# Four blocks on one core: the first two weight chunks of a layer split ahead, row blocks transposed at the old layer's end

## What is computed

```python
for l in range(2):                       # the hybrid layers
    h = rms_norm(x, pre_g[l])
    p = h @ w_in[l] + b_in[l]            # 16 column groups
    mix = concat(stick_breaking(p), sparse(p), forgetting(p), latent(p)) * silu(gates)
    x = x + rms_norm(mix @ w_out[l], post_g[l])
x = x + attention_ab(rms_norm(x, ln_ab) @ w_in_ab) @ w_out_ab
x = x + attention_c(rms_norm(x, ln_c) @ w_in_c) @ w_out_c
return rms_norm(x, ln_f)
```

## Time and profile before

| what | value |
|---|---|
| time, three runs | median 1887.13 us (1882.69 to 1889.14) |
| time of the profiled execution | 1885.34 us |
| its span, first to last instruction | 1883.3 us |
| its mean granted TensorE clock | 0.996 |
| TensorE matmul busy | 1857.6 us, 99% |
| VectorE busy | 1011.1 us, 54% |
| ScalarE busy | 859.5 us, 46% |
| DMA | 338.99 MB, mean 180 GB/s |

### The profile page before, as it was taken

How to read it: one execution, slowest core, us unless ns; L and a number is a source line. 1 busy time by engine, 2 the same in 40 slices (tenths; PEclk the granted TensorE clock), 3 DMA queues, 4 the chain that set the end, 5 groups by cost and what they waited for, 6 DMA issues and landing times.

```text
span 1883.3 us, 22540 instructions
## 1 busy us (share of the span) xinstructions
PE 1857.6 (99%) x9566; PEld 1590.7 (84%) x9566; DVE 1011.1 (54%) x987; ACT 859.5 (46%) x1066; POOL 163.2 (9%) x168
## 2 busy tenths in 40 slices
PE   8999999999999999999999999999999999999998
PEld 6889988898788998889878888888888888888886
DVE  5545454474663455457465555455455555555544
ACT  5344443464543445346445443354354434435443
POOL 2300011000340001000020000010000101100011
PEclk9999999999999999999999999999999999999999
DMA  9665555455566455446556555455556555456553
GB/s 313 201 193 153 157 189 169 145 182 190 191 203 205 144 172 191 149 140 205 170 176 197 183 192 189 161 184 175 182 179 200 179 167 184 146 172 201 174 184 112
DMA packets 187156, 338.99 MB, mean 180 GB/s; under 512 B 6848, under 2 KB 48688, under 8 KB 186160
## 3 DMA queue, kind: packets, MB, share of 16 engines
q1 hardware_dynamic: 181536, 316.89, 51.8%
q0 software_dynamic: 5232, 20.59, 3.9%
q10 hardware_dynamic: 288, 0.07, 0.0%
HBM read 335.43 MB, written 2.10 MB: 179 GB/s over the span
## 4 chain that ended last, share of the span: by engine, by line
PE 92%; DVE 3%; ACT 2%; DMA 1%; issue 1%; ACTq 0%; DVEq 0%
PE acc L1503 27%; PE acc L1505 27%; PE acc L1504 27%; PE bank L1656 3%; DVE w_lo L975 2%; PE bank L1596 1%; DMA raw<-in_w_in 1%; PE bank L1625 1%; PE bank L1645 1%; PE bank L1860 1%; PE bank L1586 1%; PE bank L1759 1%; ACT w_hi L641 1%; PE bank L1614 0%; DVE x L1299 0%
## 5 line engine op out<-in xcount | busy, mean ns | idle before, releaser
L975 DVE TENSOR_TENSOR w_lo<-raw,w_hi 128x2048 fp32r<-128x2048 f32 (+4 forms) x304 | 668.1, 2200 | 581.6 <-ACT w_hi L641 581.6
L1503 PE MATMUL acc<-w_hi,xt_hi 128*128 128x512 f32 (+4 forms) x2432 | 923.6, 380 | 8.5 <-DVE w_lo L975 8.3
L1505 PE MATMUL acc<-w_hi,xt_lo 128*128 128x512 f32 (+4 forms) x2432 | 915.7, 377 | 0.0
L1504 PE MATMUL acc<-w_lo,xt_hi 128*128 128x512 f32 (+4 forms) x2432 | 915.2, 376 | 0.0
L641 ACT ACTIVATE w_hi<-raw 128x2048 fp32r<-128x2048 f32 (+4 forms) x304 | 549.6, 1810 | 614.7 <-PE acc L1505 591.9
L1503 PEld LDWEIGHTS acc<-w_hi,xt_hi 128*128 128x128 f32 x2432 | 457.4, 188 | 89.4 <-DVE w_lo L975 7.0
L1505 PEld LDWEIGHTS acc<-w_hi,xt_lo 128*128 128x128 f32 x2432 | 457.3, 188 | 80.7
L1504 PEld LDWEIGHTS acc<-w_lo,xt_hi 128*128 128x128 f32 x2432 | 457.6, 188 | 78.7 <-issue 0.5
L716 ACT ACTIVATE S<-S,nmax 128x256 f32<-128x256 f32 (+1 forms) x128 | 59.9, 469 | 74.9 <-DVE nmax L1067 49.9
L515 POOL DMA_DIRECT2D bias<-in_b_in x32 | 18.0, 562 | 613.8 <-DVE M L1055 209.9
L703 ACT ACTIVATE PT<-bank 128x512 f32<-128x512 f32 (+2 forms) x76 | 36.3, 554 | 69.7 <-PE bank L1645 51.8
(11 more groups left out here) (279 smaller groups left out, 1192.6 us busy)
## 6 DMA issues: line engine op xcount, KB each, us to landing
raw<-in_w_in SPq DMA_DIRECT2D x76, 1024.0 KB, 5.1
raw<-in_w_in_c SPq DMA_DIRECT2D x64, 1024.0 KB, 5.5
raw<-in_w_in_ab SPq DMA_DIRECT2D x52, 1024.0 KB, 5.1
raw<-in_w_out SPq DMA_DIRECT2D x32, 1024.0 KB, 5.1
raw<-in_w_out_ab SPq DMA_DIRECT2D x16, 1024.0 KB, 5.0
raw<-in_w_out_c SPq DMA_DIRECT2D x16, 1024.0 KB, 5.0
raw<-in_w_in SPq DMA_DIRECT2D x16, 688.0 KB, 4.0
raw<-in_w_in SPq DMA_DIRECT2D x16, 576.0 KB, 3.8
```

The costliest lines, as they stand in the source:

```text
L975: nc.vector.tensor_tensor(w_lo[r][:, :, 0:n], raw[r][:, :, 0:n], w_hi[r][:, :, 0:n].bitcast(F32), ALU.subtract).then_inc(lo_done.s, 1)
L1503: nc.tensor.matmul(s, xt_hi[:, kt, rows], w_hi[r][:, k, 0:n], start=(q == 0 and k == 0), stop=False)
L1504: nc.tensor.matmul(s, xt_hi[:, kt, rows], w_lo[r][:, k, 0:n], start=False, stop=False)
L1505: ins = nc.tensor.matmul(s, xt_lo[:, kt, rows], w_hi[r][:, k, 0:n], start=False, stop=(q == NQ - 1 and k == KQ - 1))
```

## The change

- The first two chunks of layers 1 and 2 (AB) get places of their own, `ahead`. Pair 0 lies in the memory of `TQ, TK, TV, CT`, pair 1 in that of `QT, KT, ukv, QR, mla_g`. They may be written when the old layer's last slot has done its first step. Their splits move from the last slot's stages to those of the slot before it. The other chunks go on through the ring of three.
- The loads of `mla_g` and `ukv`, whose memory pair 1 uses, move behind the first slot on GpSimd's queue, in both hybrid layers.
- Row blocks (0, 2) and (0, 3) are transposed at the end of the old layer's last slot.
- The first slot does all four chunks for t = 0, then all four for t = 1. The blocks of t = 1 are transposed after its steps 2, 3 and 4 (counted from 0).
- On ScalarE and VectorE the row blocks stand elsewhere between norm, x updates and splits.

```diff
+AHEAD = 2
...
+        def ahead_pair(i):
+            with ExitStack() as scope:
+                return [scope.enter_context(nc.sbuf_tensor(f"ahead_{part}{i}", [P, KQ, CW], F32R)) for part in ("hi", "lo")]
...
         w_lo = [sb(f"w_lo{r}", [P, KQ, CW], F32R) for r in range(RING)]
+        ahead = [ahead_pair(0)]
         TQ, TK, TV = sb("TQ", [P, T, GW]), sb("TK", [P, T, GW]), sb("TV", [P, T, GW])
         CT = sb("CT", [P, T, GW])
...
+        ahead.append(ahead_pair(1))
         with ExitStack() as hybrid:
...
-        def must_be_used(i):
-            j = i - RING
-            return j + 1 - min(max(j + 1 - NQ * CMP_SLOT, 0), NQ)
+        def weights(turn, i):
+            if turn and i < AHEAD:
+                return ahead[i]
+            r = (i - AHEAD * turn) % RING
+            return w_hi[r], w_lo[r]
+        def place_free(turn, i):
+            if turn and i < AHEAD:
+                return split_used(turn, -RING)
+            used = i + 1 - RING - (AHEAD if turn and i < AHEAD + RING else 0)
+            if turn < DEPTH:
+                used -= min(max(used - NQ * CMP_SLOT, 0), NQ)
+            return split_used(turn, used)
...
-        SPLITS_AFTER = {-1: NQ - 1, CMP_SLOT - 1: NQ - 2, CMP_SLOT: NQ + 2, H_SLOTS - 2: NQ - 2, H_SLOTS - 1: RING}
+        SPLITS_AFTER = {-1: NQ - 2, CMP_SLOT - 1: NQ - 2, CMP_SLOT: NQ + 2, H_SLOTS - 2: NQ - 2 + AHEAD, H_SLOTS - 1: NQ - AHEAD}
...
-        FIRST_SLOT = [(q, (t,)) for t in range(T) for q in range(RING)] + EVENLY[RING:]
+        FIRST_SLOT = [(q, (t,)) for t in range(T) for q in range(NQ)]
...
@@ gpsimd
+                nc.gpsimd.dma_start(fbias[:, :], ...)
+                nc.gpsimd.dma_start(uq, ...)
+                pool.wait_ge(*tr_lo(l, 8))
+                nc.gpsimd.dma_start(gT[:, :], ...)
+                next_bias(0)
                 nc.gpsimd.dma_start(mla_g[:, 0:MLA_QR], all_rows(q_g[bass.ds(l, 1), :])).then_inc(small_in.s, 16)
                 nc.gpsimd.dma_start(mla_g[:, MLA_QR:GW], all_rows(kv_g[bass.ds(l, 1), :])).then_inc(small_in.s, 16)
-                nc.gpsimd.dma_start(fbias[:, :], ...)
-                nc.gpsimd.dma_start(uq, ...)
                 nc.gpsimd.dma_start(ukv[:, :], flat(w_ukv)).then_inc(mlaw_in.s, 16)
-                pool.wait_ge(*tr_lo(l, 8))
-                nc.gpsimd.dma_start(gT[:, :], ...)
-                next_bias(0)
...
@@ scalar, split_hi
-                r = i % RING
+                hi, _ = weights(turn, i)
                 act.wait_ge(*arrived(turn, i))
-                act.wait_ge(*split_used(turn, must_be_used(i) if turn is not DEPTH else i + 1 - RING))
-                nc.scalar.activation(w_hi[r][:, :, 0:n], raw[r][:, :, 0:n], ACT.Copy).then_inc(hi_done.s, 1)
+                act.wait_ge(*place_free(turn, i))
+                nc.scalar.activation(hi[:, :, 0:n], raw[i % RING][:, :, 0:n], ACT.Copy).then_inc(hi_done.s, 1)
...
@@ scalar and vector, first_rows
-                rows_t(turn, 0, 3)
-                for v in range(3):
-                    rows_t(turn, 1, v)
+                rows_t(turn, 1, 0)
+                rows_t(turn, 1, 1)
                 yield
+                rows_t(turn, 1, 2)
                 rows_t(turn, 1, 3)
-                yield
...
@@ scalar, hybrid_after, last slot of a layer
+                            if t == 0:
+                                row_root(l, t, "eps6")
+                            rows_t(l + 1, 0, 2 * t)
+                            rows_t(l + 1, 0, 2 * t + 1)
                             if t:
-                                yield
-                            row_root(l, t, "eps6")
-                            for v in range(2 if t == 0 else 0):
-                                yield
-                                rows_t(l + 1, 0, v)
-                            if t:
-                                rows_t(l + 1, 0, 2)
+                                row_root(l, t, "eps6")
+                            yield
...
@@ vector, hybrid_after, last slot of a layer
                         output_mean(l, t, 1e-6)
+                        if t:
+                            rows_t(l + 1, 0, 2)
+                            rows_t(l + 1, 0, 3)
                         output_norm(l, t)
                         for v in range(2):
+                            if t and v:
+                                yield
                             d = slice(CW * v, CW * v + CW)
                             nc.vector.scalar_tensor_tensor(x[:, t, d], M[:, t, d], stat[:, 14 + t:15 + t], x[:, t, d],
                                                            ALU.mult, ALU.add).then_inc(x_done.s, 1)
-                            if t and v == 0:
-                                rows_t(l + 1, 0, 2)
-                                yield
...
-                        for v in range(2 if t == 0 else 0):
+                        if t == 0:
+                            rows_t(l + 1, 0, 0)
+                            rows_t(l + 1, 0, 1)
                             yield
-                            rows_t(l + 1, 0, v)
...
@@ tensor, layer_starts
-                for v in range(2):
+                for v in range(N_OUT):
                     drained[v] = tr_lo(turn, v + 1)
...
-                after = {0: some((0, 2), (0, 3)), 1: some((1, 0)), 2: some((1, 1), (1, 2)), 3: some((1, 3))}
+                after = {2: some((1, 0)), 3: some((1, 1), (1, 2)), 4: some((1, 3))}
...
@@ tensor, last slot of a layer
-                        halfway, after = {step: lambda: rows_t(l + 1, 0, 0)}, {step: lambda: rows_t(l + 1, 0, 1)}
+                        def last_rows():
+                            rows_t(l + 1, 0, 2)
+                            rows_t(l + 1, 0, 3)
+                        halfway = {step: lambda: rows_t(l + 1, 0, 0)}
+                        after = {step: lambda: rows_t(l + 1, 0, 1), step + 1: last_rows}
```

More of the change, by code:

```diff
@@ L537, in _ @@
                 next_bias(0)
+                nc.gpsimd.dma_start(mla_g[:, 0:MLA_QR], all_rows(q_g[bass.ds(l, 1), :])).then_inc(small_in.s, 16)
+                nc.gpsimd.dma_start(mla_g[:, MLA_QR:GW], all_rows(kv_g[bass.ds(l, 1), :])).then_inc(small_in.s, 16)
+                nc.gpsimd.dma_start(ukv[:, :], flat(w_ukv)).then_inc(mlaw_in.s, 16)
                 rope(TQ[:, :, :].rearrange("p t (h n) -> p t h n", n=HD), "rope", P,
@@ L875, in _ @@
             for l in range(DEPTH):
-                i = RING if l else PIECED
+                i = NQ
                 for k in range(-1, H_SLOTS):
-                    todo = SPLITS_AFTER.get(k, NQ) + (RING - PIECED if l == 0 and k == -1 else 0)
+                    todo = SPLITS_AFTER.get(k, NQ)
                     for _ in hybrid_after(l, k):
@@ L946, in _ @@
             for turn, (_, _, slot0, slots, stages, _, _) in zip((DEPTH, DEPTH + 1), SECTIONS):
[L947 removed]
+                i = NQ * slot0 + (RING if turn > DEPTH else NQ)
                 last = N_CHUNKS2 if turn == DEPTH + 1 else 10 ** 9
                 for k in range(-1, len(slots) + N_OUT):
[L950 removed]
+                    todo = {-1: NQ - (1 if turn > DEPTH else 2), len(slots) + N_OUT - 1: 1}.get(k, NQ)
                     for _ in att_after(turn, k, slots, stages):
@@ L1502, in slot @@
                             s = acc[a % 2][t][:, 0:n]
-                            nc.tensor.matmul(s, xt_hi[:, kt, rows], w_hi[r][:, k, 0:n], start=(q == 0 and k == 0), stop=False)
-                            nc.tensor.matmul(s, xt_hi[:, kt, rows], w_lo[r][:, k, 0:n], start=False, stop=False)
-                            ins = nc.tensor.matmul(s, xt_lo[:, kt, rows], w_hi[r][:, k, 0:n], start=False,
+                            nc.tensor.matmul(s, xt_hi[:, kt, rows], hi[:, k, 0:n], start=(q == 0 and k == 0), stop=False)
+                            nc.tensor.matmul(s, xt_hi[:, kt, rows], lo[:, k, 0:n], start=False, stop=False)
+                            ins = nc.tensor.matmul(s, xt_lo[:, kt, rows], hi[:, k, 0:n], start=False,
                                                    stop=(q == NQ - 1 and k == KQ - 1))
@@ L1510, in slot @@
                         ins.then_inc(split_used.s, 1)
-                    elif q == NQ - 1:
+                    elif q == NQ - 1 and order is LAST_SLOT:
                         ins.then_inc(rows_done.s, 1)
```

22 lines of the change are left out of this document (9 added, 13 removed).

## The result

The changed kernel takes **1878.17 us** (median of 4 runs, 1877.12 to 1879.30), beside 1887.31 for the kernel before (4 runs, 1882.69 to 1889.14): ratio **0.9958**, 95% interval 0.9946 to 0.9970. Run again on another occasion it took 1879.24 (5 runs) beside 1885.01 (21 runs of the kernel before): ratio 0.9968, 0.9956 to 0.9981. So it is faster by 0.3 to 0.4%. The profiled execution took 1878.3 us, its span is 1876.5; before they were 1885.34 and 1883.3. The trace thus holds 7.0 us in time and 6.8 in span, and those have to be placed.

The account below looks back on a forecast made before the run. TensorE, busy 99% of the span, was taken as the bound, leaving only its waits and slow clock to win. Boundaries 6.35 us plus start 1.2 made 7.6, so 1879.5 us against the median, range 1873 to 1887.

Parts of the forecast that it names:

- Case A: Whole kernel: boundaries gain 6.35 us and the start 1.2, giving 1879.5 us, own range 1873 to 1882; chance 0.57.
- rival B: First slot: VectorE stands behind GpSimd's multiply and add, TensorE waits 1.7 us; 1881.7, or 1885.1 with clock lost; chance 0.20.
- start, the wait at 49: First layer's second slot: with ukv's load moved, the 1.22 us low-part wait goes, gaining 1.2 us, bounds 0 and 1.22.
- first boundary, gain: End of first layer: waits and slow clock fall from 4.2 us to 1.05.
- second boundary, gain: End of second layer: waits and slow clock fall from 4.1 us to 0.9.
- wait at the first block (square late): Old layer's end: square some 0.3 us late, so TensorE waits 0.15 us at the first boundary, none to 0.15 at the second.
- wait before the fourth step: First slot: TensorE waits 0.6 us for chunk 3's low part, bounds nothing and 1.7 us.
- gap before the seventh step: First slot: block (1,2) ready late behind chunk 4's low part, 0.3 us, bounds 0 and 1.1.
- The price of the boundary before: Old kernel's layer boundaries: low-part waits plus 1.72 us of slow clock cost 4.2 and 4.1 us, together 8.3.
- rival C: Old layer's end: ScalarE is held by the second early load landing late, from about 7 us; 1895 us; chance 0.10.
- the low part of chunk 3: First slot, VectorE: 2.34 us behind a 1.63 us x update, done at 501.5 where TensorE asks at 500.9.
- D: After the first slot or at the start: gain given back, only one part stays, 1.2 us, 1885.9; chance 0.13.

Follow-up runs that it names:

- e1: Kernel before with only the loads of mla_g and ukv moved behind the first slot on GpSimd: 1883.93 us, ratio 0.9992.
- e5: Changed kernel, but GpSimd begins its x update of row tile 1 only after chunk 3's low part: 1876.41 us, repeated at 1877.01.
- e7: Changed kernel with one more GpSimd multiply, result unused, ahead of its update of row tile 1: 1877.92 us in one run.
- e3: Changed kernel with the splits of chunks 0 and 1 back among the last slot's stages: 1894.40 us, ratio 1.0048.
- e2: Changed kernel with the first slot's old order, chunks 0 to 2 per row tile, then chunk 3: 1892.78 us, ratio 1.0040.
- e6: Changed kernel with GpSimd's later update, plus all four row-tile-1 blocks before chunk 4's split on ScalarE and VectorE: 1876.43 us, ratio 0.9955.
- e4: Changed kernel with row blocks (0,2) and (0,3) transposed after the new slot's first step again: 1885.02 us, ratio 0.9997.

## Why the prediction was right, point by point

**The forecast case.** 1879.5 us was said against the median of the kernel before, 7.6 us less; the median is 1878.17, and the profiled span gives 6.8. That the time came within 1.3 us owes something to the base: by medians the gain is 9.1 us on the first occasion and 5.8 on the second, where the kernel before had 1885.01. The forecast of 7.6 lies between them. Case A happened in its boundaries and its clock, but one of its steps went as rival B had it, as is said below. The table of the steps is:

| step of the sum | forecast | measured |
|---|---|---|
| start, the wait at 49 | 1.2 | 1.39 (alone, in `e1`: 1.38) |
| first boundary, gain | 3.15 | 2.93 |
| second boundary, gain | 3.2 | 2.53 |
| wait at the first block (square late) | 0.15 | none seen (square 0.03 late) |
| wait before the fourth step | 0.6 | 1.00 and 0.99 |
| gap before the seventh step | 0.3 | 0.23 |

**The price of the boundary before was right.** The 2.3 us waits and the slow clock are what went. The second boundary's 1.72, which I had only carried over from the first, can be counted: eight starts from 982.37 to 985.89 in 3.52 us where 1.82 would do, 1.70. By the waits the second boundary should have given 4.04 less 1.22, 2.8 us; it gave 2.53, and the last 0.3 I can't place.

**The early splits were priced right, their lateness too high.** The second load landed about 4.9 us after its issue, against the 5.1 I took, so its high part began at 477.78, that is 479.17 on the time scale of before (1.39 added) and not 479.4. That is most of why the square was 0.03 instead of 0.3 us late. That rival C's condition (a landing over 7 us) was far off is seen in the 1.07 us wait before the second high part.

**The term that was mis-sized: the low part of chunk 3.** I gave it 2.34 us, so 0.6 of wait, on the ground that "the same two instructions meet the same two of GpSimd as before". They did not: before, the four row-block instructions stood between the update and the low part, and GpSimd's add (to 498.92) was over when the low part began, 498.74, but for 0.2 us. Now the low part comes directly behind the update, at 497.35, with GpSimd's add just begun (496.95 to 498.57), and has 3.38 us. The wait was 1.00. The range of that term, 0 to 1.7, held it.

It was luck that the miss stayed so small. A low part 1.04 us longer than forecast should have made the wait 1.6, above the 1.39 up to which I had seen the clock kept. On the time scale of before the x update began at 497.18 and not at 497.5, and TensorE asked at 501.17 and not at 500.9; these two took 0.6 us off again.

**The reading that was wrong: how the two engines meet.** I argued from the overlap of the records that VectorE and GpSimd "slowed each other rather than queue". `e5` and `e7` show that they queue. The record of an instruction that stands behind the other engine's has its wait inside: the x update is 0.74 us of work (0.75 in `e5`) in a record of 1.63, and the low part is 2.28 in one of 3.38. Two records that overlap say nothing about sharing. The ends in the changed kernel go the same way as in `e7`: multiply 496.87, update 497.42 (0.55 later, as there), add 498.57 (1.15, as there), low part 500.73 (2.16, there 2.14). In the kernel before, too, the multiply ends at 497.23 and the update at 497.78, 0.55 later: the rows that I read as sharing held the turns.

The Trainium skill (SBUF — State Buffer, on port contention) states that a VectorE instruction with two SBUF inputs and a GpSimd instruction that reads SBUF exclude each other for a whole instruction. It was right where my row reading spoke against it: the low part of 3.38 in the changed kernel, 2.28 in `e5` and 3.12 in `e7` agree with it.

So rival B named the mechanism and case A did not. B let the low part begin at the end of GpSimd's add, about 500.3, and end at 502.6. On the same time scale the add ended at 499.96 and the low part at 502.12. B's price was 0.7 us too dear, a wait of 1.7 for 1.00: the low part ended 0.48 earlier than B had it, and TensorE asked 0.27 later. With 1.00 the clock stayed, and the time came out on A's side.

**The clock.** The forecast took it that waits of 1.22 and 1.39 us keep the clock and 2.32 lose it. In the changed kernel this held: 1.00 us of wait, clock 1.00 behind both. As a rule it is too strong: 1.84 us lost it in `e3`, 2.02 kept it in `e2`, 2.32 kept it once in `e1`, and the 1.39 us at 590 to 600 lost it in `e5`, in its repeat and in `e6`, and kept it in the other eight profiles (before, changed, again, `e1`, `e2`, `e3`, `e4`, `e7`). The step of the prediction that was exposed to this is the 2 x 1.72 us of its gain. The prediction's sign of a clock of 1.00 throughout held at the boundaries only: the fall at 222, which the kernel before has too, is still there.

**The rivals.** C did not happen: the square was not late. D did not: between the boundary and 591 TensorE has no idle record, and what was gained at the first boundary is still there at the second. The whole of the 6.8 us stays to the end.

**What may lie beyond.** `e5` (1876.41 and 1877.01 us) and `e6` (1876.43) have no boundary wait. In spans they are 1874.1 to 1875.6 against 1876.5 and 1877.2 of the changed kernel; in medians 1 to 3 us under it, with overlapping intervals (ratios 0.9956 and 0.9957 against 0.9958 and 0.9968). That they are faster is therefore not shown in time; that the waits are gone is. Against that stands a clock that falls at 592 in all three profiles of this kind, some 1.5 us each. Why it falls there once the boundary has no wait is open: three profiles with it and eight of the other kernels without look like more than luck, but nothing was run to tell what links the two. A next step would be to take away the 1.39 us wait in the compression slot, which every kernel here still has.

## What to carry to other kernels

A wait at a layer's boundary that has VectorE or ScalarE at its end can be cured by giving the first tiles of the next layer a place of their own and preparing them where those engines are idle, but only together with an order that then needs little of the work that can't be early: here the change without the moved row blocks gained nothing, and without the early splits it lost 9 us. Each of `e2`, `e3` and `e4` takes one part out of an order that was written for the whole, so they show that the parts need each other as written, and not the most that each could give alone. Where VectorE's two-input instructions meet GpSimd's, read neither record as work; count turns, and give the non-urgent GpSimd instruction a wait of its own. Price a wait on TensorE as its length plus, at some odds, a slow clock behind it, and look for the clock in each profile at all places, since a fall at one can hide what was gained at another.
